# First attention of a two-layer trunk, worked by pairs of heads: values in 512-column chunks, q and k in squares of four tiles, three of eight of them in seven products

## The chip, the cores and the metric

The kernel runs on one core of one Trainium2 chip. The metric is the device time of one execution in microseconds. Three runs of the kernel before took 2495.29, 2496.64 and 2497.62 us; the median is 2496.64.

## The reference

A trunk of two layers on x of 256 positions and 2048 channels, all in float32. Layer 0 mixes tokens with differential attention, layer 1 with a dilated window attention; each is followed by a gated feed-forward block with a convolution of width 3. The change is in layer 0's attention alone:

```python
qkv = h @ w_qkv                      # 256 x 2048 by 2048 x 6144; h = rmsnorm(x)
q, k, v = jnp.split(qkv, [nqk, 2 * nqk], axis=-1)     # nqk = 2048
q = rmsnorm(q.reshape(B, S, N_HEADS, 2, HEAD_DIM), q_gain)   # 8 heads, 2 maps, 128
k = rmsnorm(k.reshape(B, S, N_HEADS, 2, HEAD_DIM), k_gain)
v = v.reshape(B, S, N_HEADS, V_DIM)                          # 256 a head
...
logits = jnp.einsum('bqhme,bkhme->bhmqk', qb, k) * scale + bias[:, None]
logits = jnp.where(dist >= 0, logits, NEG)
p = jax.nn.softmax(logits, axis=-1)
a = p[:, :, 0] - lam_full * p[:, :, 1]
... jnp.einsum('bqhk,bkhe->bqhe', a, v)
o = rmsnorm(o, subln_g) * (1.0 - lam_init)
return o.reshape(B, S, ATTN_WIDTH) @ w_o
```

## The kernel before, in words

**Products.** A float32 product is made of three matmuls on a fast type: a number is the sum of a high part and a low part, and high by high, low by high and high by low are added up. The 256 positions are two blocks (m = 0, 1) of 128. xT holds x transposed, in both parts. Weights come in chunks through four slots: SyncE issues the load into w_raw, ScalarE makes the high part w_hi (`split`, `split_up`, `split_b`; "hi split" below), VectorE subtracts to get w_lo ("lo split"), and TensorE multiplies. A chunk's raw slot is loaded anew when its low part is made (`free_slot`), its high part is overwritten when TensorE has used the chunk (`used`). Each engine has one list of instructions and works it in order, so where an instruction stands in it is part of the schedule.

**Chunks.** A plain chunk of 2048 columns costs TensorE 24 matmuls of 512 columns. In the up and down projections and in the second attention, chunks are "squares": 256 rows of x by 1024 columns of weights in four tiles. A square with 24 matmuls is `std`. For the rows in MIXED, pairs 4 to 6 of eight, a square is done in seven products in place of eight (Strassen's scheme in Winograd's form): an entry `one` of 9 matmuls from three of the loaded tiles, and an entry `sum` of 12 from four tiles that VectorE adds up (`sum_tiles`, three operations) in another slot, with no load of its own. These use mixed blocks of x (`mix_x`, `mix_high`, `mix_low`), and their products gather in four banks of PSUM that are combined after the last (`combine`).

**The first attention, before** (`a_head`, per head h, eight heads, the middle six in a loop). Chunks 0 to 3 are q and k of one head, 4 x 128 columns by 512 rows, 24 matmuls of 512 columns each. Chunks 4 to 7 are its v, 256 columns, 24 matmuls of 256 columns each. q and k gather in banks 0 and 1, v in banks 2 and 3, the attention's own results in banks 4 to 7. While a head's chunks run, the attention of the head before is done in between, by `a_attend` at the chunks in A_STEPS = (0, 2, 3, 6): scores after chunk 0; transposes of the differences of probabilities after chunk 2; P x V after chunk 3; transposes of the normed output after chunk 6. q and k of the head itself are transposed after chunk 7. VectorE adds bias, takes the maximum and, behind ScalarE's exponentials, subtracts the two maps (`a_softmax`). The norms of o and of the next head's q and k share one chain of inverse root (`a_norms`).

**The second attention** (`b_head`) has four plain chunks and eleven entries of squares, the list THREE, per head: 279 matmuls of 512 columns.

**After the last head** the output projection (`out_proj`) has 16 chunks of 24 matmuls; chunk j of the first eight needs head j of oT, in two parts (`split_o` on ScalarE and VectorE). The last head's attention is done in between, at A_LAST_STEPS = (0, 2, 3, 5).

## Time and profile before

| | us |
|---|---|
| median of three runs | 2496.64 |
| the profiled execution, span from its first to its last instruction | 2494.1 |
| TensorE busy in the span | 2487.8 |
| VectorE busy | 2100.0 |
| ScalarE busy | 1464.0 |
| GpSimd busy | 44.3 |

The profile gives the profiled execution's span; what lies around it is not in it. The median of the runs is 2.5 us longer than the span. TensorE's granted clock is 9 or more tenths of full speed in all of 40 equal slices. The 16 DMA engines move 491 MB, at 197 GB/s in the mean. The chain that ended last runs on TensorE for 98% of the span. The first attention lies at about 10 to 312 us of the span, its output projection from there to about 402, the heads of the second attention at about 1113 to 1680.

### The profile page before, as it was taken

To read this page: it belongs to the slowest core of one execution; us is meant where nothing else is said; L and a number is where in the kernel's file an instruction comes from. 1 tells how busy PE (TensorE), PEld (TensorE's weight loads), DVE (VectorE), ACT (ScalarE), POOL (GpSimd) and SP (SyncE) were. 2 spreads that over 40 slices of the span, in tenths; PEclk is the share of its full clock that TensorE was granted. 3 is DMA by queue.
4 is the path that set the end of the run, shared out by engine and by line. 5 is a ranking of instruction groups with operands and counts; after the bars stand their busy time and mean duration, and the time that the engine had idled before them with its cause. 6 is when DMAs were issued, how large, how long until landed. Compare 5 with 4: busy or idle time off the path is not lost.

```text
span 2494.1 us, 30623 instructions
## 1 busy us (share of the span) xinstructions
PE 2487.8 (100%) x11823; PEld 2088.7 (84%) x11823; DVE 2100.0 (84%) x2387; ACT 1464.0 (59%) x1561; POOL 44.3 (2%) x54
## 2 busy tenths in 40 slices
PE   9999999999999999999999999999999999999999
PEld 8988888888888888888888888888888888888887
DVE  6656666999999999998778878776699999999998
ACT  5545555766767566556545545545566676766654
POOL 1000000000000000000000000000000000000000
PEclk9999999999999999999999999999999999999999
DMA  8554554757667557476556666654476666755754
GB/s 283 180 164 162 177 198 139 247 192 248 207 214 225 193 187 244 169 227 196 157 161 188 188 190 195 185 164 152 149 251 204 220 221 206 234 186 200 240 174 159
DMA packets 364820, 491.16 MB, mean 197 GB/s; under 512 B 19285, under 2 KB 216101, under 8 KB 362256
## 3 DMA queue, kind: packets, MB, share of 16 engines
q1 hardware_dynamic: 360448, 465.64, 56.5%
q0 software_dynamic: 4000, 23.63, 4.3%
q8 instruction: 86, 1.41, 0.2%
q14 instruction: 46, 0.38, 0.0%
q10 hardware_dynamic: 240, 0.10, 0.0%
HBM read 468.31 MB, written 3.68 MB: 189 GB/s over the span
## 4 chain that ended last, share of the span: by engine, by line
PE 98%; DVE 1%; ACT 0%; DMA 0%; issue 0%; ACTq 0%
PE psum L1945 43%; PE psum L1949 22%; PE psum L1831 8%; PE psum L1832 8%; PE psum L1838 8%; PE psum L2048 2%; PE psum L1958 1%; PE psum L1957 1%; PE psum L1956 1%; PE psum L2175 1%; PE psum L1787 0%; PE psum L2139 0%; PE psum L2173 0%; PE psum L2147 0%; PE psum L2159 0%; DVE w_lo L1116 0%
## 5 line engine op out<-in xcount | busy, mean ns | idle before, releaser
L1945 PE MATMUL psum<-w_hi,xT 128*128 128x512 f32 x3936 | 984.7, 390 | 0.0
L666 ACT ACTIVATE w_hi<-w_raw 128x2048 fp32r<-128x2048 f32 (+1 forms) x350 | 631.5, 1810 | 397.3 <-PE psum L1949 262.8
L1945 PEld LDWEIGHTS psum<-w_hi,xT 128*128 128x128 f32 x3936 | 736.6, 188 | 151.8
L1116 DVE TENSOR_TENSOR w_lo<-w_raw,w_hi 128x2048 fp32r<-128x2048 f32 (+1 forms) x332 | 705.3, 2145 | 55.7 <-ACT w_hi L666 55.4
L1949 PE MATMUL psum<-w_lo,xT 128*128 128x512 f32 x1968 | 516.0, 389 | 0.1
L1949 PEld LDWEIGHTS psum<-w_lo,xT 128*128 128x128 f32 x1968 | 369.3, 188 | 77.5 <-DVE w_lo L1116 1.0
L1831 PE MATMUL psum<-w_hi,xT 128*128 128x512 f32 (+1 forms) x1008 | 362.0, 369 | 0.0
L1832 PE MATMUL psum<-w_hi,xT 128*128 128x512 f32 (+1 forms) x1008 | 355.9, 363 | 0.0
L1124 DVE TENSOR_TENSOR w_lo<-w_raw,w_hi 128x2048 fp32r<-128x2048 f32 (+1 forms) x118 | 255.7, 2179 | 41.0 <-ACT w_hi L679 40.6
L679 ACT ACTIVATE w_hi<-w_raw 128x2048 fp32r<-128x2048 f32 (+1 forms) x118 | 215.3, 1830 | 102.7 <-PE psum L1949 63.1
L1945 PE MATMUL psum<-w_hi,mixT 128*128 128x512 f32 x896 | 239.6, 389 | 0.0
L1106 DVE TENSOR_TENSOR w_lo<-w_raw,w_hi 128x2048 fp32r<-128x2048 f32 (+1 forms) x98 | 188.7, 1941 | 58.6 <-ACT w_hi L655 58.1
L1838 PE MATMUL psum<-w_lo,xT 128*128 128x512 f32 (+1 forms) x1008 | 221.8, 362 | 0.0
L1831 PEld LDWEIGHTS psum<-w_hi,xT 128*128 128x128 f32 x1008 | 190.3, 189 | 29.0 <-DVE phase L1613 0.3
L1832 PEld LDWEIGHTS psum<-w_hi,xT 128*128 128x128 f32 x1008 | 190.4, 189 | 28.6
L1838 PEld LDWEIGHTS psum<-w_lo,xT 128*128 128x128 f32 x1008 | 174.2, 189 | 29.3
L1945 PEld LDWEIGHTS psum<-w_hi,mixT 128*128 128x128 f32 x896 | 168.2, 188 | 35.0
L655 ACT ACTIVATE w_hi<-w_raw 128x2048 fp32r<-128x2048 f32 (+1 forms) x98 | 157.4, 1630 | 20.0 <-PE psum L1838 7.7
L1142 DVE TENSOR_TENSOR w_raw<-w_raw 128x1024 f32<-128x1024 f32 x112 | 136.4, 1218 | 3.5 <-DMA w_raw<-in_f_w_down 3.2
L1949 PE MATMUL psum<-w_lo,mixT 128*128 128x512 f32 x448 | 138.0, 389 | 0.0
L1949 PEld LDWEIGHTS psum<-w_lo,mixT 128*128 128x128 f32 x448 | 84.1, 188 | 17.5
L882 ACT ACTIVATE phase<-psum,conv 128x256 f32<-128x256 f32 x176 | 82.3, 571 | 5.4 <-PE psum L2048 5.2
(201 smaller groups left out, 1919.1 us busy)
## 6 DMA issues: line engine op xcount, KB each, us to landing
w_raw<-in_f_w_up SPq DMA_DIRECT2D x352, 512.0 KB, 5.1
w_raw<-in_f_w_down SPq DMA_DIRECT2D x176, 512.0 KB, 5.1
w_raw<-in_b_w_qkv SPq DMA_DIRECT2D x192, 256.0 KB, 3.9
w_raw<-in_a_w_qkv SPq DMA_DIRECT2D x94, 512.0 KB, 4.4
w_raw<-in_b_w_qkv SPq DMA_DIRECT2D x256, 128.0 KB, 2.6
w_lo<-w_raw POOLq DMA_DIRECT2D x18, 1024.0 KB, 7.0
w_raw<-in_a_w_o SPq DMA_DIRECT2D x16, 1024.0 KB, 5.1
w_raw<-in_b_w_qkv SPq DMA_DIRECT2D x32, 512.0 KB, 6.2
```

What stands on the lines that cost most here:

```text
L655: nc.scalar.activation(w_hi[:, slot, 0:width], w_raw[:, slot, 0:width], ACT.Copy).then_inc(hi_ready, 1)
L666: nc.scalar.activation(w_hi[:, slot, cols], w_raw[:, slot, cols], ACT.Copy).then_inc(hi_ready, 1)
L679: nc.scalar.activation(w_hi[:, slot, cols], w_raw[:, slot, cols], ACT.Copy).then_inc(hi_ready, 1)
L1106: nc.vector.tensor_tensor(w_lo[:, slot, 0:width], w_raw[:, slot, 0:width], w_hi[:, slot, 0:width], ALU.subtract).then_inc(lo_ready, 1)
L1116: nc.vector.tensor_tensor(w_lo[:, slot, cols], w_raw[:, slot, cols], w_hi[:, slot, cols], ALU.subtract).then_inc(lo_ready, 1)
L1124: nc.vector.tensor_tensor(w_lo[:, slot, cols], w_raw[:, slot, cols], w_hi[:, slot, cols], ALU.subtract).then_inc(lo_ready, 1)
L1142: chain.step(nc.vector.tensor_tensor(t[:, 0:2, :], b[:, 1::2, :], b[:, 0:1, :].to_broadcast([P, 2, 512]), ALU.add))
L1831: pe.matmul(o, xh, hi, start=(first and i == 0), stop=False)
L1832: pe.matmul(o, xl, hi, start=False, stop=False)
L1838: ins = pe.matmul(psum[:, banks[m], 0:n], xT[:, k, 0, P * m:P * (m + 1)], lo, start=False, stop=(last and i == len(blocks) - 1))
L1945: pe.matmul(o, x[:, h, P * m:P * (m + 1)], hi, start=start and h == 0, stop=False)
L1949: return pe.matmul(o, x[:, 0, P * m:P * (m + 1)], part_of(w_lo, c % SLOTS, 512 * tile, 512), start=False, stop=stop)
```

## The change

The eight heads are worked as four pairs. For each pair (`a_pair`) there are 15 entries: four plain chunks "all" that hold v of both heads, 512 columns by 512 rows; then squares for q and k of both heads, whose four tiles are 256 rows by the 512 columns of one head and the 512 of the other. Squares 4, 5 and 6 of eight are done as `one` and `sum`. A pair's own banks and the other four change places with each pair; v gathers in two of the own banks, then the squares in all four, and the attention of the pair before works in the other four until the `one` and `sum` products of this pair need them.

The attention (`a_attend`) is now done for two heads at once, at A_STEPS = (2, 3, 5, 6, 8): transposes of q and k after entry 2, scores after 3, transposes of the differences after 5, P x V after 6, transposes of the normed output after 8. The first `sum` entry (entry 10) waits until both takes of oT are done. In the output projection the steps of the last pair are (1, 2, 4, 4, 5), and chunks 6 and 7 need its two last heads. The loop over heads is gone from every engine's list. The norms of o have their own inverse root. The mixed blocks of x are made for the first attention too, in the first pair.

```diff
+A_ENTRIES = tuple(("all", j) for j in range(4)) + (
+    ("std", 0), ("std", 1), ("std", 2), ("one", 4), ("std", 3), ("one", 5), ("sum", 4), ("sum", 5), ("one", 6), ("sum", 6),
+    ("std", 7))
...
-A_STEPS = (0, 2, 3, 6)
-A_LAST_STEPS = (0, 2, 3, 5)
+A_STEPS = (2, 3, 5, 6, 8)
+A_LAST_STEPS = (1, 2, 4, 4, 5)
```

ScalarE:

```diff
+            def a_attend(j, p, steps, base):
+                if j == 0:
+                    a_squares(p)
                 if j == steps[0]:
+                    a_take_q(p, base)
                 if j == steps[1]:
+                    a_exp(p)
+                if j == steps[2]:
+                    a_take_aT(p, base)
                 if j == steps[3]:
+                    a_square_o(p, base)
+                    a_norm_o(p, base)
+                if j == steps[4]:
+                    a_take_oT(p, base)
```

VectorE:

```diff
+            def a_attend(j, p, steps, base):
+                if j == 0:
+                    a_norm(p)
                 if j == steps[0]:
+                    a_take_k(p, base)
+                if j == steps[1]:
+                    a_softmax(p, base)
+                if j == steps[1] + 1:
+                    a_subtract(p)
                 if j == steps[3]:
+                    dve.wait_ge(a_osq_ready, p + 1)
+                    rsqrt(o_r, o_ss, o_t, [(slice(0, 4), 1.0 / VD)], a_o_rstd)
+                if j == steps[4]:
+                    dve.wait_ge(a_to, p + 1)
+                    nc.vector.tensor_scalar(a_oT[:, 4 * p + 1:4 * p + 4:2, :],
...
+            def a_pair(c, p, odd):
+                for e in range(A_PAIR):
+                    if p == 0 and e < 2:
+                        take_xT(0, G_MIX, 2 + e)
+                        split(c + e + LEAD)
+                    if e == 3:
+                        a_take_v(c + e, p, odd)
+                    if e + LEAD + 1 == A_ONES[0]:
+                        add_weights(c + A_ONES[0], c + A_SUMS[0])
+                    if p > 0 or e > 0:
+                        split_ahead(c, e, AO0)
+                    for one, to in zip(A_ONES[1:], A_SUMS[1:]):
+                        if e + LEAD + 2 == one:
+                            add_weights(c + one, c + to)
+                    if p == 0:
+                        begin(0, G_MIX, e)
...
+                            mix_x(0)
...
                     else:
+                        a_attend(e, p - 1, A_STEPS, 4 - 4 * odd)
+                    if p == A_PAIRS - 1 and e == 11:
+                        for hd in range(4):
+                            split_o(a_oT, hd)
+                    if e == A_PAIR - 2:
+                        a_combine(c + A_SUMS[-1], p, odd)
+                    if e == A_PAIR - 1:
+                        a_sum(c + e, p, odd)
```

TensorE:

```diff
+                if what == "std" and j == 0:
+                    def lower_free():
+                        pe.wait_ge(a_v_act, p + 1)
+                        pe.wait_ge(a_v_dve, p + 1)
...
+                    if e == A_SUMS[0] and p > 0:
+                        pe.wait_ge(a_oT_act, p)
+                        pe.wait_ge(a_oT_dve, p)
+                    a_entry_of(c + e, e, p, odd)
...
+                        a_attend(e, p - 1, A_STEPS, 4 - 4 * odd)
```

`split_ahead(c, e, end)` makes the part of entry e + 3. How the rows stand on an engine, at the places of which the prediction speaks:

VectorE before, from the scores of one head to the differences (a_diff) and the next lo split; L1299 and L1302 add the bias, L1321 makes the differences.

```order
L1302 SCALAR_TENSOR_TENSOR phase<-psum,phase 128x256
L1306 TENSOR_REDUCE small<-phase 128x2 [waits a_lg_ready]
L1307 TENSOR_REDUCE small<-phase 128x2
L252 ISA
L1309 TENSOR_SCALAR small<-small 128x4 [waits dve_chain]
L1311 RECIPROCAL small<-small 128x4 [waits a_probs]
```

VectorE in the changed kernel, the same place for a pair; L1318 to L1321 take the maxima, L1139 to L1144 add up weights for entry 10, L1121 is the lo split of entry 7, L1325 is where the subtraction begins.

```order
L1318 TENSOR_REDUCE small<-phase 128x4 [waits a_lg_ready]
L1319 TENSOR_REDUCE small<-phase 128x4
L1321 TENSOR_SCALAR small<-small 128x8 [waits dve_chain]
L1139 TENSOR_TENSOR w_raw<-w_raw 128x1024 [waits w_lo_ready,w_in2]
L1142 TENSOR_TENSOR w_raw<-w_raw 128x512 [waits dve_chain]
L1144 TENSOR_TENSOR w_raw<-w_raw 128x512 [waits dve_chain]
L1121 TENSOR_TENSOR w_lo<-w_raw,w_hi 128x1536 [waits w_hi_ready]
L1325 RECIPROCAL small<-small 128x8 [waits a_probs]
L1327 TENSOR_SCALAR small<-small,nlam 128x4 [waits dve_chain]
```

Between the maxima and the reciprocal, which waits for the exponentials, stand four operations on weights that were behind the subtraction before. ScalarE in the changed kernel, from the exponentials (L756) through the squares of o (L771), its scaling (L779) and the hi splits (L678) to the take of oT (L785).

```order
L756 ACTIVATE phase,small<-phase,small 128x256 x3
L756 ACTIVATE phase,small<-phase,small 128x128 x4
L678 ACTIVATE w_hi<-w_raw 128x1536 [waits w_used,w_in2]
L678 ACTIVATE w_hi<-w_raw 128x2048 [waits w_used,w_in3]
L763 ACTIVATE phase<-psum 128x768 [waits a_ta]
L678 ACTIVATE w_hi<-w_raw 128x1536 [waits w_used,w_in0]
L771 ACTIVATE phase,small<-psum 128x256 [waits a_pv]
L771 ACTIVATE phase,small<-psum 128x256 x3
L779 ACTIVATE phase<-psum,small 128x256 [waits a_o_rstd]
L779 ACTIVATE phase<-psum,small 128x256 x3
L678 ACTIVATE w_hi<-w_raw 128x2048 [waits w_used,w_sum_ready] x2
L785 ACTIVATE phase<-psum,sub_g 128x2x256 [waits a_to]
```

The hi split of entry 7 (1536 columns) stands right behind the exponentials, and the hi splits of entries 10 and 11 between the scaling and the take. VectorE from the end of the inverse root of o to its take of oT (L1354).

```order
L1121 TENSOR_TENSOR w_lo<-w_raw,w_hi 128x2048 [waits w_hi_ready] x2
L1139 TENSOR_TENSOR w_raw<-w_raw 128x1024 [waits w_lo_ready,w_in3]
L1142 TENSOR_TENSOR w_raw<-w_raw 128x512 [waits dve_chain]
L1144 TENSOR_TENSOR w_raw<-w_raw 128x512 [waits dve_chain]
L1354 TENSOR_SCALAR phase<-psum,sub_g 128x2x256 [waits a_to]
```

The take stands behind two lo splits (entries 10 and 11) and the sum for entry 13. VectorE at the start, behind the inverse root of x: before, then in the changed kernel (L1264 and L1258 are the first take of q and k, and of v).

```order
L1723 COPY gains<-psum 128x10 [waits pe_setup,r_rstd]
L1725 COPY conv<-psum 128x352 x2
L1106 TENSOR_TENSOR w_lo<-w_raw,w_hi 128x1024 [waits w_hi_ready]
L1733 ISA phase,small<-phase 128x128 [waits lam_in]
L1733 ISA small 128x1
L1733 ISA phase,small<-phase 128x128
L1733 ISA small 128x1
L1737 TENSOR_SCALAR sub_g<-gains 128x2 [waits consts_ready]
L1740 TENSOR_SCALAR nlam<-small 128x1 [waits lam_exp]
L1264 TENSOR_SCALAR phase<-psum,small 128x512 [waits w_used,lam_ready]
```

```order
L1743 COPY gains<-psum 128x10 [waits pe_setup,r_rstd]
L1745 COPY conv<-psum 128x352 x2
L1153 TENSOR_TENSOR phase<-phase 128x384 [waits xT_hi]
L1154 TENSOR_TENSOR phase<-phase 128x384
L1156 TENSOR_TENSOR phase<-phase 128x384 [waits dve_chain]
L1158 TENSOR_TENSOR phase<-phase 128x384 [waits dve_chain]
L1258 TENSOR_SCALAR phase<-psum,small 128x512 [waits w_used]
L1121 TENSOR_TENSOR w_lo<-w_raw,w_hi 128x2048 [waits w_hi_ready]
```

The four mixing operations stand ahead of the take now, and the take is of v.

## Rows read from the trace of the kernel before

**Rows 1.** The table by stage: a head of the first attention, one of the second (columns: stretch and its length; then for PE, PEld, DVE, ACT, POOL busy us (instructions); clock, DMA share, GB/s).

```profile
86.40:124.04 37.64, 37.64 (x225) 33.46 (x223) 23.29 (x39) 19.47 (x43) 0.00 (x0) 1.00 0.52 168
1269.50:1341.08 71.58, 71.58 (x337) 60.01 (x336) 56.56 (x62) 36.70 (x32) 2.38 (x2) 1.00 0.61 178
```

**Rows 2.** PE in order of time: start, length, line, operands.

```profile
82.96 0.28 PE L1831 MATMUL psum<-w_hi,xT 128*128 128x256 f32 x1
83.08 0.28 PE L1832 MATMUL psum<-w_hi,xT 128*128 128x256 f32 x1
...
86.94 0.40 PE L1831 MATMUL psum<-w_hi,xT 128*128 128x512 f32 x1
87.17 0.40 PE L1832 MATMUL psum<-w_hi,xT 128*128 128x512 f32 x1
```

**Rows 3.** DVE in order of time, within one head of the first attention.

```profile
131.24 0.69 DVE L1299 SCALAR_TENSOR_TENSOR phase<-psum,phase 128x512 f32<-128x512 f32 x1 [2.10 <-PE psum L1864]
...
133.34 0.17 DVE L1309 TENSOR_SCALAR small<-small 128x4 f32<-128x4 f32 x1
135.45 0.18 DVE L1311 RECIPROCAL small<-small 128x4 f32<-128x4 f32 x1 [1.94 <-ACT phase L767]
...
137.25 3.43 DVE L1106 TENSOR_TENSOR w_lo<-w_raw,w_hi 128x2048 fp32r<-128x2048 f32 x2
...
152.58 0.24 DVE L1197 TENSOR_SCALAR small<-small 128x8 f32<-128x8 f32 x2 [1.83 <-ACT phase L745]
```

**Rows 4.** ACT in order of time, within the same head.

```profile
133.55 0.51 ACT L763 ACTIVATE phase<-phase,small 128x256 f32<-128x256 f32 x1 [6.73 <-DVE small L1309]
...
135.32 2.85 ACT L655 ACTIVATE w_hi<-w_raw 128x2048 fp32r<-128x2048 f32 x2
...
151.73 0.36 ACT L745 ACTIVATE phase<-psum 128x256 f32<-128x256 f32 x1
...
152.44 1.05 ACT L655 ACTIVATE w_hi<-w_raw 128x1024 fp32r<-128x1024 f32 x1
155.11 0.84 ACT L780 ACTIVATE phase<-psum,small 128x256 f32<-128x256 f32 x2 [1.62 <-DVE small L1211]
155.84 3.72 ACT L655 ACTIVATE w_hi<-w_raw 128x2048 fp32r<-128x2048 f32 x2
```

**Rows 5.** DVE in order of time, within one head of the second attention.

```profile
1359.13 4.09 DVE L1124 TENSOR_TENSOR w_lo<-w_raw,w_hi 128x1536 fp32r<-128x1536 f32 x2 [0.30 <-ACT w_hi L679]
1363.15 1.22 DVE L1142 TENSOR_TENSOR w_raw<-w_raw 128x1024 f32<-128x1024 f32 x1
...
1365.73 0.42 DVE L1671 COPY phase<-psum 128x256 f32<-128x256 f32 x1
```

**Rows 6.** DVE in order of time, in the first head.

```profile
30.76 1.23 DVE L1106 TENSOR_TENSOR w_lo<-w_raw,w_hi 128x1024 fp32r<-128x1024 f32 x1 [1.09 <-ACT w_hi L655]
...
34.55 0.95 DVE L1725 COPY conv<-psum 128x352 f32<-128x352 f32 x2
...
37.58 0.75 DVE L1264 TENSOR_SCALAR phase<-psum,small 128x512 f32<-128x512 f32 x1
```

**Rows 7.** PE in order of time, the end of the fourth chunk.

```profile
34.22 1.98 PE L1838 MATMUL psum<-w_lo,xT 128*128 128x512 f32 x8
```

**Rows 8.** Instructions of one line: the mixing of x.

```profile
L1156 DVE TENSOR_TENSOR phase<-phase x3: 547/548/548, 416.9 to 1792.9; 128x384 f32<-128x384 f32 x3
```

**Rows 9.** PE in order of time, at the start.

```profile
1.20 4.41 PE L2261 MATMUL psum<-phase 128*128 128x128 f32 x22 [1.20 <-DVE phase L1744]
6.48 0.63 PE L1787 MATMUL psum<-ident,resid 128*128 128x128 f32 x4 [0.87 <-DMA resid<-in_x]
...
8.07 1.50 PE L2261 MATMUL psum<-phase 128*128 128x128 f32 x12
```

**Rows 10.** The table by stage, the end of the span.

```profile
2491.00:2493.00 2.00, 0.00 (x0) 0.00 (x0) 0.64 (x1) 0.00 (x0) 0.00 (x0) 1.00 0.59 224
2493.00:2494.10 1.10, 0.00 (x0) 0.00 (x0) 0.00 (x0) 0.00 (x0) 0.00 (x0) 0.54 0.19 69
```

More of the change, by code:

```diff
@@ L28 @@
 import math
-from contextlib import ExitStack, contextmanager
+from contextlib import ExitStack
 import numpy as np
@@ L95 @@
 A0 = 0
-AO0 = A0 + H * A_HEAD
+AO0 = A0 + A_PAIRS * A_PAIR
 UP0 = (AO0 + OUT, 0)
@@ L145, in loads_of @@
     if A0 <= c < AO0:
-        return 2 if (c - A0) % A_HEAD < 4 else 1
+        return {"all": 1, "sum": 0}.get(kind(c), 4)
     if B0 <= c < BO0:
@@ L469, in load_x, with free_slot, load_a_pair @@
                 sp.dma_start(resid[:, :, cols], src).then_inc(x_in[q], 16)
-            def free_slot(c, more=None):
-                if more is None:
-                    lo_made(sp, c - SLOTS)
-                else:
-                    at_least(sp, lo_ready, c - SLOTS + 1 + more)
-            def load_a_head(c, h, more=0):
-                for j in range(A_HEAD):
-                    first = isinstance(h, int) and j < 4
+            def free_slot(c):
+                lo_made(sp, c - SLOTS)
+            def load_a_pair(c, p):
+                for e, (what, j) in enumerate(A_ENTRIES):
+                    if what == "sum":
+                        continue
+                    first = p == 0 and e < 4
@@ L647, in _, with split @@
         def _(act):
-            def split(c, more=0, width=W, rate=RATE):
+            def split(c):
                 if c >= END:
@@ L839, in out_proj @@
                     split(c + j + LEAD)
-                    if j < 5:
-                        split_o(oT, oT_act, oT_dve, j + 2)
-                    if j == 3 and n == 1:
-                        a_squares(H)
-                    attend(j, H - 1, steps)
+                    if early + j < H - group:
+                        split_o(oT, oT_act, oT_dve, early + j, group)
+                    attend(j, last, steps, base)
                     if j == steps[-1]:
-                        split_o(oT, oT_act, oT_dve, H - 1)
+                        for hd in range(H - group, H):
+                            split_o(oT, oT_act, oT_dve, hd, group)
                     if j == 7:
@@ L1098, in _, with split @@
             chain = Chain(dve, dve_chain)
-            def split(c, more=0, width=W):
+            def split(c):
                 if c >= END:
@@ new lines, in a_sum, with a_norm @@
+            def a_sum(c, p, odd):
+                chunk_used(dve, c)
+                dve.wait_ge(a_combined, p + 1)
+                for i in range(2 * M):
+                    nc.vector.tensor_tensor(a_raw[:, i, :], psum[:, a_bank(odd) + i, :], a_raw[:, i, :],
+                                            ALU.add).then_inc(a_summed, 1)
+            def a_norm(p):
+                dve.wait_ge(a_sq_ready, p + 1)
+                rsqrt(q_r, q_ss, q_t, [(slice(0, 16), 1.0 / HD)], None)
+                chain.settle()
+                r = q_r.rearrange("p (g m s) -> p g m s", m=M, s=4)
+                chain.step(nc.vector.tensor_tensor(
+                    r, r, r_r.unsqueeze(1).unsqueeze(3).to_broadcast([P, 2, M, 4]), ALU.mult))
+                chain.settle()
+                v = a_raw.rearrange("p m (s e) -> p (m s) e", e=HD)
+                nc.vector.tensor_tensor(v, v, q_r.unsqueeze(2).to_broadcast([P, 16, HD]), ALU.mult).then_inc(a_qkn, 1)
@@ L1366, in a_head @@
-                    if j == 7:
-                        a_take_v(c + j, h, more)
-                        split(c + j + LEAD, more)
-                        a_take_k(h)
+                            mix_low(0)
+                    else:
+                        a_attend(e, p - 1, A_STEPS, 4 - 4 * odd)
+                    if p == A_PAIRS - 1 and e == 11:
+                        for hd in range(4):
+                            split_o(a_oT, hd)
+                    if e == A_PAIR - 2:
+                        a_combine(c + A_SUMS[-1], p, odd)
```

680 lines of the change are left out of this document (319 added, 361 removed).

## The prediction

> **What bounds the kernel now.** I read the table by stage first. Over one head of the first attention TensorE is busy for all of its 37.64 us, VectorE for 23.29 and ScalarE for 19.47; over one head of the second attention TensorE is busy for all of 71.58 us and VectorE for 56.56 [rows 1]. So TensorE's own work is the whole time, and every wait that others keep from it is worth nothing until it grows past its cover. The second view is the order of matmuls in time, for the distance from one start to the next: 0.12 us at 256 columns and 0.23 at 512 [rows 2]; over a run of 512-column matmuls I use 0.227. The third is the order in time of VectorE and ScalarE within one head [rows 3, 4] and in one head of the second attention [rows 5], for the pieces of the chains that the change makes longer.
>
> **What TensorE saves.** The value projections were 192 matmuls of 256 columns for two heads and become 96 of 512: 192 x 0.120 - 96 x 0.227 = 1.25 us a pair. Q and k were 192 matmuls of 512 columns for two heads; now five plain squares of 24, three "one" entries of 9 and three "sum" entries of 12 make 183: 9 x 0.227 = 2.04 us. Together 3.3 us a pair, 13.2 us over four pairs. The attention's own small matmuls stay the same in number. Half of the interludes go, which I cost at 0.1 to 0.5 us in all and leave out. Had the 256-column matmul been as fast per column as the 512-column one, 0.114 instead of 0.12, the first term would be zero and the sum 8.2.
>
> **Steady pairs: the softmax chain.** Let 0 be the end of the scores of the pair before. PE (its entries 4 and 5) then has 2 x 24 x 0.227 = 10.9 us of weights' work before it asks for the differences (a_diff). What it asks for takes, with everything that stands in the queues between:
> VectorE's lo split of entry 6 ends 0.45 us after the scores, because it had to stand behind the take of v;
> two softmax fronts, 2 x (133.34 - 131.24) = 4.2 us [rows 3];
> two sets of exponentials on ScalarE, 2 x (135.32 - 133.55) = 3.55 us [rows 4];
> then ScalarE's hi split of entry 7 (1536 columns, three quarters of 3.72/2, so 1.4) [rows 4] and VectorE's lo split of the same (4.02 to the next start for one of 1536 and one of 2048, so 1.75 and 2.25) [rows 5]: both stand ahead of the subtraction in VectorE's list, and the hi stands behind the exponentials in ScalarE's;
> two subtractions, 2 x (137.25 - 135.45) = 3.6, less the reciprocal and one small multiply that do not double, 2.9 us [rows 3].
> The sum is 14.2 us against 10.9: TensorE waits 3.3 us. The weight sum for entry 10 (2.58 us, [rows 5]) lies beside the exponentials and costs nothing. Before, one head's chain (6.0 us from 131.24 to 137.25) had the same cover.
>
> **Steady pairs: the output chain.** From the end of P x V TensorE has entry 7 (9 matmuls, 2.04), entry 8 (24, 5.45), eight transposes (0.9; one comes 0.11 after another, from 12 in 1.50 [rows 9]) and entry 9 (2.04) = 10.4 us until entry 10, which waits for a_oT_dve. The chain: 0.25 to notice; four squares of o, 2 x (152.44 - 151.73) = 1.4 [rows 4]; the inverse root, 155.11 - 152.58 = 2.5 [rows 3, 4]; four scalings, 2 x (155.84 - 155.11) = 1.5 [rows 4]; hi split of entry 10, 3.72/2 = 1.86 [rows 4]; lo splits of 10 and 11, 2 x 2.25 [rows 5]; the weight sum for entry 13, 1365.73 - 1363.15 = 2.58 [rows 5]; and only then the take of oT by VectorE, 0.75, as the 512-column take from PSUM in [rows 6]. That is 15.3 us: TensorE waits 4.9. The transposes in the middle are met: the scaling ends 5.7 us after P x V, TensorE comes at 7.5.
>
> Both waits come once in pairs 1, 2 and 3: 3 x (3.3 + 4.9) = 24.6 us. A 1024-column operation might cost anything from one head's time to twice it; with softmax front and subtraction at 1.7 instead of 2 the waits are 0.3 x 3.9 = 1.2 us a pair less, and with 0.1 us more at each of some ten handovers 1 us more: 21 to 28 us.
>
> **The first pair.** Its values lie in banks 0 and 1, which the lower half of entry 4 overwrites, so TensorE waits there for VectorE's take of v. Before, the take of the first chunks' result ended at 38.3 (37.58 + 0.75) [rows 6] and the next chunk, in other banks, did not need it. Ahead of it stands the inverse root of x, which started at 32.0 behind a lo split (30.76 + 1.23) [rows 6]. Now ScalarE makes six extra copies of x (0.4 each, about 1 us of them outside its idle time) and two full hi splits in place of half ones (1.9), and the last lo split is full too (1.1): the root starts near 36. Then the root, 2.5 [rows 3, 4]; the constants, 0.95 [rows 6]; four new mixing operations of 0.55 [rows 8]; the take, 0.75: 42.4. TensorE ends the fourth chunk at 34.22 + 8 x 0.227 = 36.0 as before [rows 7] and has 12 matmuls (2.7 us) that need no bank of v: a wait of 3.7 us, say 4, between 2 and 6.
>
> **The last attention,** inside the output projection, has the steps 1, 2, 4, 4, 5. The softmax chain is as above with a hi and lo split of 2048 columns: 4.1 us of wait. Differences and P x V share a step, so the take of the transposed probabilities is bare, 1.1. Its first chunk waits for the combination, pushed back by four split_o on VectorE, and the transposes of q and k for their norms: 1.5. Chunk 6 needs oT of the same step: the rest of a hi split 0.95, a lo split 2.2, take 0.75, split_o on both engines (512 columns, 0.65 each, a little under the take) 1.3 = 5.2; before, a chunk lay between. The o norms lack 0.4. Together 12 us, between 7 and 15.
>
> **The clock.** In the stages of [rows 1] TensorE never waits, and the granted clock is 1.00. In its last stretch TensorE does nothing for 2 us from 2491 and the granted clock is then 0.54 [rows 10], its lower level (1.2 GHz) for nearly all of it. At the start 22 warming matmuls take 4.41 us where 12 take 1.50 once it is warm, so 22 would take 2.6: the climb costs 1.8 us [rows 9]. All nine large waits (4.0; 3 x 3.3 and 3 x 4.9; 4.1 and 5.2) are longer than 2 us. I charge 1.8 to the six long ones and half to the three of 3.3: 13.5 us, between 0 and 18.
> The Trainium skill, "TensorE: Matmul & The Clock Gate", section "HAM oscillation — how this bites in real kernels", says that a kernel which keeps TensorE waiting between bursts pays the climb again in every round; the last stretch agrees that idleness lowers the clock, but no wait inside this kernel shows it. By the page the charge is the upper end, 9 x 1.8 = 16 us; without it zero.
>
> **The sum,** against the profiled execution (span 2494.1; the median of the timed runs, 2496.6, lies 2.5 above it, and I put that on top): 2494.1 - 13.2 + 24.6 + 4 + 12 + 13.5 + 2.5 = 2537.5. Work of the other engines elsewhere, loads (the same bytes) and the later stages I cost at nothing: VectorE is at 79% in the second attention's heads with the same split and sum entries, and TensorE doesn't wait there.
>
> **Rivals.**
> A. The waits come, the clock stays up: 2524. For it: 0.87 us of idleness near the start did not bring the lower level back (the matmuls behind it are not slower) [rows 9]. Against it: 2 us at the end did.
> B. Only part of the waits. Were oT taken in time, by VectorE's queue running ahead of what I add up, 3 x (4.9 + 1.8) = 20 us go: 2517. Against it: the list is in order, and the take stands behind both lo splits and the sum.
> C. All is covered, as in the second attention: 2494.1 - 13.2 + 2.5 = 2483. For it: the same form of head runs there without a wait. Against it: there one head's softmax, not two heads', stands in each step, and oT is taken right after P x V with no norm between.
> D. VectorE becomes the bound of whole pairs: 46.6 us for two heads before, plus 7.7 for three weight sums, up to 6 for eight combining operations of at most 0.75, and 2.5 for a second inverse root, is about 63 of 72; were gaps in its order to cost 5 us a pair over my sum: 2552.
>
> **Chances.** Forecast 0.5; A 0.2; B 0.12; D 0.08; C 0.1. The range from 2508 to 2550 leaves out C and part of D. About 0.2% (5 us) is what a measurement of this kernel can tell from no change. Faster comes with C alone: 0.08; within 0.2%, with half of the waits of B and no fall of the clock: 0.03; slower: 0.89. Should it be faster, C's condition decides: both waits of a steady pair under 1 us.
>
> **What would show it.** A pair of heads lasts 3.3 us less than 75.3 with no waits, 80 to 84 with them. PE's idle time is led by the transposes of the differences, released by VectorE's subtraction, and by the first sum entry, released by the take of oT, three times each, then by entry 4 of the first pair and by chunk 6 of the output projection. The matmuls behind a wait stand 0.43 apart if the clock fell. If TensorE's idle time in the first attention is under 10 us, my chains are wrong; if it is 40 and the time 2524, only the clock is.

## The result, and the profile after

The changed kernel takes 2544.5 us (median of four runs, 2541.1 to 2545.9); the kernel before, on the same chip, 2496.0 (2495.2 to 2497.6). The ratio is 1.0193, with a 95% interval of 1.0179 to 1.0208. The forecast was 2537.5, between 2508 and 2550.

The page of the kernel after, its engines and its chain:

```profile
PE 2496.5 (98%) x11403; PEld 2075.8 (82%) x11403; DVE 2155.9 (85%) x2389; ACT 1484.1 (58%) x1544; POOL 44.3 (2%) x54
...
PE 92%; DVE 4%; ACT 2%; issue 1%; DMA 1%; SPq 0%; ACTq 0%; DVEq 0%
```

TensorE's busy time has grown by 8.7 us, though products were taken from it, and is still 98% of a span of 2543.9 us. Of the chain it holds 92% where it held 98%, so the page hints at the loss but does not place it. All of the loss comes ahead of the first gated feed-forward block. VectorE's first mixing of x for that block, before and then after, starts 49.7 us later, and the whole span is 49.8 us longer:

```profile
416.94 0.55 DVE L1156 TENSOR_TENSOR phase<-phase 128x384 f32<-128x384 f32 x1
```

```profile
466.60 0.55 DVE L1153 TENSOR_TENSOR phase<-phase 128x384 f32<-128x384 f32 x1
```

The table of waits shows where, for TensorE over the first 430 us (engine, line it waited at, what released it; us in all, times, longest):

```profile
PE psum L1979 <- issue: 14.4, 3, 4.8
PE psum L1882 <- DVE phase L1335: 12.7, 4, 3.7
PE psum L1990 <- DVE conv L1745: 5.6, 1, 5.6
PE psum L1846 <- DVE xT L1400: 5.1, 1, 5.1
PE psum L1866 <- DVE phase L1291: 2.1, 1, 2.1
...
PE psum L1888 <- ACT phase L763: 0.9, 1, 0.9
```

In the order of the rows: the first sum entry of pairs 1 to 3, which waits for the transposed o (the releaser is not named here; the rows of VectorE below do it); the transposes of the softmax differences, three times 3.0 in pairs and once 3.7 beside the output projection; entry 4 of the first pair; chunk 6 of the output projection; the last transposes of q and k; the last transposed probabilities. They are 40.8 us. Two more, of 0.5 us behind the last pair and 0.2 us at the transposes of the last o, bring them to 41.5; 2.0 us of waits at the very start, which the kernel before has too (2.4 there), are not counted. In the kernel before, TensorE was busy for the whole of a head [rows 1]. Now, in the table by stage, pairs 1 and 2 (each from its q and k transposes to the next pair's), and the stretch behind the wait for o in pair 1:

```profile
100.83:186.61 85.78, 77.97 (x339) 64.27 (x338) 60.05 (x79) 43.18 (x80) 0.00 (x0) 0.92 0.46 148
186.61:269.15 82.54, 74.72 (x339) 61.80 (x338) 60.05 (x79) 43.19 (x80) 0.00 (x0) 0.96 0.47 153
151.00:157.80 6.80, 6.16 (x15) 4.83 (x16) 4.41 (x3) 2.43 (x2) 0.00 (x0) 0.50 0.91 305
```

Pair 1 lasts 85.78 us and pair 2 82.54; two heads took 2 x 37.64 = 75.28 [rows 1]. In pair 2 TensorE is busy for 74.72 us, at 0.96 of the clock: only one of its two waits brought the clock down. In pair 1 both did. The third row lies at 0.50 for its whole length. What that does to a matmul, and what the wait looks like, is seen in TensorE's order of time at that place:

```profile
151.65 2.90 PE L1979 MATMUL psum<-w_hi,mixT 128*128 128x512 f32 x6 [4.80 <-issue]
154.34 1.05 PE L1979 MATMUL psum<-w_hi,xT 128*128 128x512 f32 x2
```

The wait is 4.80 us (in brackets). Behind it six matmuls of 512 columns take 2.90 us, where at full clock they start 0.23 apart [rows 2]. VectorE at the same time:

```profile
143.80 4.49 DVE L1121 TENSOR_TENSOR w_lo<-w_raw,w_hi 128x2048 fp32r<-128x2048 f32 x2 [3.44 <-ACT w_hi L678]
148.21 1.22 DVE L1139 TENSOR_TENSOR w_raw<-w_raw 128x1024 f32<-128x1024 f32 x1
...
150.80 0.74 DVE L1354 TENSOR_SCALAR phase<-psum,sub_g 128x512 f32<-128x512 f32 x1
```

Two lo splits in one row, the three operations of a weight sum (the first is shown), and only then the take of the transposed o (L1354), which ends at 151.54: 0.1 us later TensorE goes on. This is the row for row form of the chain that was added up ahead. The other chain, on VectorE, for the softmax of the same pair:

```profile
120.17 1.76 DVE L1121 TENSOR_TENSOR w_lo<-w_raw,w_hi 128x1536 fp32r<-128x1536 f32 x1 [2.49 <-ACT w_hi L678]
121.84 0.20 DVE L1325 RECIPROCAL small<-small 128x8 f32<-128x8 f32 x1
...
122.21 1.00 DVE L1331 TENSOR_SCALAR phase<-phase,small 128x128 f32<-128x128 f32 x4
123.25 1.40 DVE L1335 SCALAR_TENSOR_TENSOR phase<-phase,small 128x128 f32<-128x128 f32 x4
```

The lo split of entry 7 stands ahead of the reciprocal and the subtractions, which end at 124.65; TensorE goes on at 124.7.

In the first pair the releaser is not the one that I had named. VectorE there:

```profile
37.28 0.15 DVE L1215 TENSOR_REDUCE small<-small 128x2 f32<-128x8 f32 x1
...
39.92 0.95 DVE L1745 COPY conv<-psum 128x352 f32<-128x352 f32 x2
...
42.91 0.74 DVE L1258 TENSOR_SCALAR phase<-psum,small 128x512 f32<-128x512 f32 x1
```

The order is: split of entry 5, inverse root from 37.28, the copy of the constants (the last of it L1745) which ends at 40.87, four mixing operations (in the gap), and the take of v at 42.91. TensorE's entry 4 starts at 40.93, 0.06 us behind the copy.

### The profile page after: what moved, and what is told of

It is laid out like the page before. It is cut to its first block, busy times and chain, and to the rows that moved or that the text cites. A ratio compares the mean times of both kernels' runs of the same rounds, so it can differ in the third digit from the quotient of the medians.

```text
span 2543.9 us, 29223 instructions
## 1 busy us (share of the span) xinstructions
PE 2496.5 (98%) x11403; PEld 2075.8 (82%) x11403; DVE 2155.9 (85%) x2389; ACT 1484.1 (58%) x1544; POOL 44.3 (2%) x54
## 4 chain that ended last, share of the span: by engine, by line
PE 92%; DVE 4%; ACT 2%; issue 1%; DMA 1%; SPq 0%; ACTq 0%; DVEq 0%
PE psum L1979 46%; PE psum L1983 23%; PE psum L1846 5%; PE psum L1847 5%; PE psum L1853 5%; PE psum L2082 2%; PE psum L1990 1%; PE psum L1992 1%; PE psum L1991 1%; PE psum L2209 1%; DVE w_lo L1121 1%; DMA w_raw<-in_a_w_qkv 1%; ACT phase L756 0%; PE psum L2173 0%; PE psum L2207 0%
## 5 line engine op out<-in xcount | busy, mean ns | idle before, releaser
L1979 PE MATMUL psum<-w_hi,xT 128*128 128x512 f32 x4264 | 1073.8, 392 | 0.0
L1979 PEld LDWEIGHTS psum<-w_hi,xT 128*128 128x128 f32 x4264 | 801.4, 189 | 165.5
L665 ACT ACTIVATE w_hi<-w_raw 128x2048 fp32r<-128x2048 f32 (+1 forms) x350 | 631.0, 1809 | 397.1 <-PE psum L1983 254.9
L1113 DVE TENSOR_TENSOR w_lo<-w_raw,w_hi 128x2048 fp32r<-128x2048 f32 (+1 forms) x332 | 705.0, 2145 | 58.4 <-ACT w_hi L665 57.6
L1983 PE MATMUL psum<-w_lo,xT 128*128 128x512 f32 x2132 | 560.3, 390 | 0.1
L1983 PEld LDWEIGHTS psum<-w_lo,xT 128*128 128x128 f32 x2132 | 400.5, 188 | 84.1 <-DVE w_lo L1113 1.0
L1121 DVE TENSOR_TENSOR w_lo<-w_raw,w_hi 128x2048 fp32r<-128x2048 f32 (+1 forms) x174 | 376.3, 2177 | 79.9 <-ACT w_hi L678 79.5
L678 ACT ACTIVATE w_hi<-w_raw 128x2048 fp32r<-128x2048 f32 (+1 forms) x174 | 316.8, 1828 | 157.5 <-PE psum L1983 100.2
L1979 PE MATMUL psum<-w_hi,mixT 128*128 128x512 f32 x992 | 270.3, 395 | 14.4 <-issue 14.4
L1846 PE MATMUL psum<-w_hi,xT 128*128 128x512 f32 x624 | 247.4, 396 | 5.7 <-DVE xT L1400 5.1
L1847 PE MATMUL psum<-w_hi,xT 128*128 128x512 f32 x624 | 244.5, 392 | 0.0
L1979 PEld LDWEIGHTS psum<-w_hi,mixT 128*128 128x128 f32 x992 | 189.3, 191 | 55.4 <-issue 15.6
L1853 PE MATMUL psum<-w_lo,xT 128*128 128x512 f32 x624 | 154.2, 389 | 0.0
L1139 DVE TENSOR_TENSOR w_raw<-w_raw 128x1024 f32<-128x1024 f32 x124 | 151.1, 1219 | 0.9 <-DMA w_raw<-in_f_w_down 0.8
L1846 PEld LDWEIGHTS psum<-w_hi,xT 128*128 128x128 f32 x624 | 118.3, 190 | 30.7 <-DVE xT L1400 5.4
L1847 PEld LDWEIGHTS psum<-w_hi,xT 128*128 128x128 f32 x624 | 118.2, 189 | 24.0
L1853 PEld LDWEIGHTS psum<-w_lo,xT 128*128 128x128 f32 x624 | 117.1, 188 | 24.3
L1103 DVE TENSOR_TENSOR w_lo<-w_raw,w_hi 128x2048 fp32r<-128x2048 f32 x38 | 86.0, 2288 | 34.1 <-ACT w_hi L654 34.1
L1142 DVE TENSOR_TENSOR w_raw<-w_raw 128x512 f32<-128x512 f32 x124 | 85.8, 692 | 4.2
L1144 DVE TENSOR_TENSOR w_raw<-w_raw 128x512 f32<-128x512 f32 x124 | 85.8, 692 | 4.2
```

Of the source, the lines that this page charges most:

```text
L665: nc.scalar.activation(w_hi[:, slot, cols], w_raw[:, slot, cols], ACT.Copy).then_inc(hi_ready, 1)
L678: nc.scalar.activation(w_hi[:, slot, cols], w_raw[:, slot, cols], ACT.Copy).then_inc(hi_ready, 1)
L1103: nc.vector.tensor_tensor(w_lo[:, slot, :], w_raw[:, slot, :], w_hi[:, slot, :], ALU.subtract).then_inc(lo_ready, 1)
L1113: nc.vector.tensor_tensor(w_lo[:, slot, cols], w_raw[:, slot, cols], w_hi[:, slot, cols], ALU.subtract).then_inc(lo_ready, 1)
L1121: nc.vector.tensor_tensor(w_lo[:, slot, cols], w_raw[:, slot, cols], w_hi[:, slot, cols], ALU.subtract).then_inc(lo_ready, 1)
L1139: chain.step(nc.vector.tensor_tensor(t[:, 0:2, :], b[:, 1::2, :], b[:, 0:1, :].to_broadcast([P, 2, 512]), ALU.add))
```

## The experiments

All are edits of the changed kernel; the comments in the edits below are the document's, and "..." stands for rows left out. "Gap" is the distance between the starts of two matmuls, which is 0.2 us or so more than the idle time in the tables. Time at the low clock is added up from the table by stage, asked for in stretches of half a microsecond over the first 430 us: it is 0 in the kernel before and 54.6 us in the changed one, in nine stretches. Each starts within one of the large waits or up to 1.5 us behind it.

**TensorE kept busy through its waits.** This version separates what the waits cost from what the clock behind them costs.

```diff
+ def spin(turns, bank):
+     for i in range(turns):
+         pe.matmul(psum[:, bank, 0:P], ident[:, :], ident[:, :], start=True, stop=True)
...
...
+ spin(15, base + 3)          # ahead of pe.wait_ge(a_diff, p + 1)
+ spin(24, 4)                 # first pair, ahead of pe.wait_ge(consts_ready, 1)
+ spin(22, 5 - 4 * odd)       # ahead of pe.wait_ge(a_oT_act, p)
+ spin(22, 5)                 # output projection, ahead of chunk 6
```

> TensorE is given idle products (fp32 identity by identity, 128 columns, written to a bank that is free) to run while it would wait: 15 calls (about 3.3 us) ahead of each wait for the subtraction of the softmax, 22 (about 4.9 us) ahead of the three waits for the transposed o of a pair and ahead of chunk 6 of the output projection, 24 (about 5.3 us) ahead of the wait for the constants in the first pair. The waits themselves stay as long as they are; only the engine is not idle in them. The wait of 2.5 us ahead of the last q and k transposes is left as it is. Theory A (the clock that falls after a wait costs about 19 us of the 50 that the change costs): eight of the nine falls are gone, one of about 3.4 us is left, and the time is 2525 to 2529 us, 1.012 of the time before. Theory B (my prediction's size of the clock term, 13.5 us, is right, and the remaining loss is longer waits): 2531 to 2533. Theory C (the clock falls whatever the engine does there, or the low clock costs nothing): 2543 to 2546, falls still at the same places.

Measured: 2526.4 us (2526.2 to 2527.3), ratio 1.0118 [1.0101, 1.0135]; no time at the low clock. TensorE at the place shown above:

```profile
142.10 5.07 PE L1860 MATMUL psum<-ident 128*128 128x128 f32 x44
147.06 1.63 PE L1988 MATMUL psum<-w_hi,mixT 128*128 128x512 f32 x6
```

The 22 calls are 44 records, 5.07 us long, and the six matmuls behind them take 1.63 us in place of 2.90. The waits are all still there, filled: no other instruction was moved. The wait ahead of the last q and k transposes was left empty (1.6 us here), and the clock stayed up behind it. This is Theory A: the clock costs 2544.5 - 2526.4 = 18.1 us and not 13.5, and the waits proper the rest. Between the two profiled executions it is 2543.9 - 2524.3 = 19.6, since that of the changed kernel was 1.2 us above its median. Rival A's picture, waits without the clock, is what this run makes, and its 2524 is 2 us from it.

**The subtraction first.**

```diff
  for e in range(A_PAIR):
+     if p > 0 and e in (4,):
+         a_attend(e, p - 1, A_STEPS, 4 - 4 * odd)
      if p > 0 or e > 0:
          split_ahead(c, e, AO0)
...
-     else:
+     elif e not in (4,):
          a_attend(e, p - 1, A_STEPS, 4 - 4 * odd)
```

> Only VectorE's order in pairs 1 to 3 changes: the subtraction of the softmax stands ahead of the split of the weights of entry 7, not behind it. Theory A (the wait of 3.4 us behind entry 5 is VectorE's order: the subtraction stood behind a 1.8 us split that itself waited for ScalarE's copy): the three waits of 3.2 us net shrink to under 0.4, TensorE comes to the next wait earlier by as much, and the wait for the transposed o stays 5.0 to 5.4, since VectorE's and ScalarE's work for it hangs on TensorE's own progress; with the falls of the clock behind two of the three waits gone the time is 2530 to 2534. Theory B (the backlog only moves: VectorE or ScalarE is what is short over the pair): the wait for o grows to about 8, the pair stays 82.4 us long and the time 2542 to 2545. Theory C (the exponentials on ScalarE end last): the wait shrinks by at most 1.5 us each, time 2539 to 2541.

Measured: 2527.6 us (2527.5 to 2528.8), ratio 1.0122 [1.0105, 1.0139]; 37.6 us at the low clock. The wait for o in the three pairs, then two waits behind the last pair:

```profile
PE psum L1981 <- issue: 14.4, 3, 4.8
...
PE psum L1868 <- DVE phase L1291: 1.6, 1, 1.6
PE psum L1848 <- DVE phase L1272: 0.9, 1, 0.9
```

The three waits for the differences are gone, and the wait for o has stayed at 4.8. Theory A, with more gained than it said: 17 us, 9 of them these waits and 0.7 the first pair's, which is 4.9 here, though the edit does not touch that pair. The low clock fell from 54.6 us to 37.6, which by the run above (18.1 us for 54.6) is worth 5.6. The remaining 1.6 us are not assigned.

**The take of o first.** The same edit with 8 in place of 4.

> Only VectorE's order in pairs 1 to 3 changes: its half of the copy of the transposed o out of PSUM stands ahead of the split of entry 11's weights and of the sums of entries 12 and 13, not behind them. Theory A (the 5.2 us wait at the first product of sums is VectorE's order; what it waits for would be ready otherwise): the three waits go to under 0.6, the falls of the clock behind them go too (2.3 us each), and the time is 2521 to 2526. Theory B (the chain of o itself is late: square, 1/sqrt, scale, transposes, with ScalarE's copy as the last): the waits shrink to about 2.6 to 3 and the clock still falls, time 2536 to 2540. Theory C (the work put off, split and sums, is then what TensorE waits for at entries 11 to 13): a new wait of 3 us or more there, time 2540 or more.

Measured: 2531.7 us (2529.5 to 2535.9), ratio 1.0141 [1.0124, 1.0158]; 37.5 us at the low clock. Waits of the three pairs and at the start of the output projection, and VectorE in order of time:

```profile
PE psum L1884 <- DVE phase L1335: 9.0, 3, 3.0
PE psum L1848 <- DVE phase L1272: 4.8, 1, 4.8
PE psum L1848 <- DVE phase L1267: 3.3, 2, 2.4
```

```profile
142.31 2.29 DVE L1121 TENSOR_TENSOR w_lo<-w_raw,w_hi 128x2048 fp32r<-128x2048 f32 x1 [3.44 <-ACT w_hi L678]
144.52 0.74 DVE L1354 TENSOR_SCALAR phase<-psum,sub_g 128x512 f32<-128x512 f32 x1
...
162.95 0.68 DVE L1267 TENSOR_TENSOR phase<-psum,phase 128x512 f32<-128x512 f32 x1
```

Theory A is right about the wait named: 14.4 us are gone, the take now stands at 144.52, between the lo splits. But 8.1 us came back at a place that none of the three theories had: the start of the chunk that follows a pair, the next pair's twice (2.4 and 0.9 us) and the output projection's once (4.8, where the changed kernel has 0.5). This chunk needs banks that VectorE must first have read for the combination (L1267 to L1272). VectorE comes to it at 162.95, behind splits for which it had waited 0.32 and 1.79 us on ScalarE. ScalarE itself was waiting for weights:

```profile
154.71 1.92 ACT L678 ACTIVATE w_hi<-w_raw 128x2048 fp32r<-128x2048 f32 x1 [0.89 <-DMA w_raw<-in_a_w_qkv]
158.79 1.92 ACT L678 ACTIVATE w_hi<-w_raw 128x2048 fp32r<-128x2048 f32 x1 [2.16 <-DMA w_raw<-in_a_w_qkv]
```

A slot is loaded anew only when its low part is made, so a low part that is late delays a load as well. How much of the 8.1 us goes this way no run takes apart. What had stood ahead of the take was put off, and TensorE, no longer held at entry 10, reached the pair's end earlier than VectorE. The gain is 12.8 us where 18 to 23 were expected.

**Both.**

> Both moves on VectorE in pairs 1 to 3: the subtraction ahead of the split of entry 7, and the copy of the transposed o ahead of the split of entry 11 and the sums. Each alone gave 17 and 13 us; in the second the wait came back at the start of the next pair (2.8, 1.3 and 5.1 us, until VectorE had combined the products of the pair before). Theory A (two waits of their own, and the new one is the splits put off, which does not grow): 17 and 13 add to 30, time 2513 to 2517. Theory B (backlog: with 3.2 us less of TensorE time ahead of it, VectorE is later yet against TensorE at the pair's end): the wait for the combine grows by up to 3 us a pair, time 2519 to 2525. Theory C (with VectorE free of it the wait at the first product of sums is the chain of o and comes back there): waits of 2.5 us there, 2519 or more.

Measured: 2520.6 us (2517.0 to 2523.8), ratio 1.0092 [1.0076, 1.0107]; 34.1 us at the low clock.

```profile
PE psum L1848 <- DVE phase L1267: 6.8, 2, 3.4
PE psum L1848 <- DVE phase L1272: 4.8, 1, 4.8
```

The gains do not add (24 us in place of 30). Theory B: the wait for the combination grew from 8.1 to 11.6 us over the three. A cause for it is in the row at 142.31 above: the lo split of entry 10 waits 3.44 us for ScalarE's high half, which stands behind the scaling of o, and this in turn behind VectorE's inverse root. That is tried below, with all the other edits.

**The constants first, in the first pair.** take_consts is called at e == 2 ahead of split_ahead and not behind the inverse root.

> First pair only: VectorE copies the constants out of PSUM before it splits the weights of entry 5, not after the 1/sqrt. My prediction held the split, the sum and the take of v responsible for a 4 us wait at entry 4; the trace after names the copy of the constants, 5.6 us. Theory A (constants): the wait ahead of entry 4 disappears, its upper half runs, and then TensorE waits for the scaled v in the middle of entry 4 for about 4.3 us, ScalarE's or VectorE's part last: total gain 1 to 2 us, time about 2543. Theory B (something else holds entry 4 at its start, a transfer or the split of its own weights): the wait at its start stays over 3 us.

Measured: 2540.1 us, one run; 41.0 us at the low clock. TensorE in entry 4:

```profile
42.67 0.47 PE L1991 MATMUL psum<-w_hi,xT 128*128 128x512 f32 x1 [4.34 <-DVE phase L1258]
```

The wait at the entry's start is gone; L1991 is in its middle, and the wait there is for the take of v (L1258), 4.34 us. Theory A, to the tenth in the wait. Of the total it said 1 to 2 us and 4.4 came: 1.3 us of wait, and the low clock is 13.6 us shorter, which by the rate above would be up to 4.5. But the changed kernel's own runs lie 4.8 us apart, so the total of one run decides little.

**Constants, inverse root and v first.** take_consts, begin and a_take_v are all called at e == 2 of the first pair ahead of the split.

> First pair only: VectorE does the constants, 1/sqrt and its half of the scaled v first, and then the split of entry 5, mix_x and the rest. Moving the constants alone left a 4.7 us gap in the middle of entry 4 until v had been copied behind mix_x (2.1 us) and the split (2.3 us). Theory A (order again): no gap over 1 us in entry 4, no low clock behind it, and the time is 4.3 us of wait plus 1.4 to 2 us of clock below the version with the constants alone: 2533 to 2536. Theory B (the split of entry 5 or the mixed x that are put off come too late): a wait of 2 us or more in entry 5 or at the first entry of mixed products, time 2538 or more.

Measured: 2536.3 us, one run; 41.0 us at the low clock. TensorE has no idle time at all between 33 and 45 us. Theory A on the wait, with a time 0.3 us above its range; of the clock nothing came back, since the one stretch that is gone here was made up by others that were longer. One run of each kernel carries no more than that.

**The tail's order.** Only the last attention, beside the output projection:

```diff
  for j in range(OUT):                       # VectorE; ScalarE with j == 5 alone
+     first = n == 1 and j in (3, 5)
+     if first:
+         attend(j, last, steps, base)
+         if j == 5:
+             for hd in range(H - group, H):
+                 split_o(oT, hd)
      split(c + j + LEAD)
...
```

> Only the last attention, beside the output projection: VectorE subtracts ahead of the split of chunk 5, and both VectorE and ScalarE copy the transposed o and split it for chunk 6 ahead of the weights of chunk 7. Theory A (order): the 4.1 us gap goes to under 0.5, the 5.4 us gap to 2.2 to 2.8 (VectorE's copy 0.75, ScalarE's 0.6 of high halves, VectorE's 0.65 of low halves and the semaphores are left), and one or two of the three clock falls go: 2 to 4 us; time 2533 to 2537. Theory B (chunk 7 is late in turn, or the exponentials end last): 2540 or more, with a new gap at chunk 7 or the old one at the transposes of the probabilities.

Measured: 2531.8 us (2531.5 to 2532.0), ratio 1.0142 [1.0126, 1.0157]; 34.1 us at the low clock, none of it behind the last pair. Waits of the tail:

```profile
PE psum L1859 <- DVE xT L1406: 2.3, 1, 2.3
PE psum L1879 <- DVE phase L1297: 1.6, 1, 1.6
```

The 3.7 us for the differences are gone, and chunk 6 waits 2.3 in place of 5.1. Theory A on the waits; the time is 1.2 us under its range of 2533 to 2537. All three falls behind the last pair are gone (17.1 us at the low clock, 5.7 by the rate above) where it had expected one or two.

**All together:** both moves in pairs 1 to 3, the constants, inverse root and v first in the first pair, and the tail's order, with ScalarE's high half of entry 10 between the squares of o and its scaling, and 9 idle products ahead of chunk 6:

```diff
  if j == steps[3]:
      a_square_o(p, base)
+     if between is not None:
+         between()                          # split_ahead(c, 7, AO0): the high half of entry 10
      a_norm_o(p, base)
```

> All moves together: both in pairs 1 to 3, ScalarE's high half of entry 10 between the squares of o and its scaling in place of behind it, constants and v first in the first pair, the tail's order, and 9 idle products (2 us) ahead of chunk 6. If every wait but the last transposes' (2.0), the probabilities' in the tail (1.1), chunk 6's (2.3) and one of about 1 a pair is gone, 43.5 us of waits come down to 9 and the low clock with them (54.6 us of it in the change, under 7 here): 2494.1 - 13.2 + 9 + 2 = 2492 in a profile, 2494 as a median, the same as before within 0.2%. Theory A (the removed products are worth their 13 us once order hides the waits): 2490 to 2497. Theory B (VectorE's backlog at the pair's end stays): 3 waits of 3 to 5 us with their clock, 2503 to 2512.

Measured: 2493.5 us (2491.9 to 2498.1, 11 runs) against 2496.5, ratio 0.9990 [0.9981, 0.9999]; 6.8 us at the low clock. Its two longest waits behind the start:

```profile
PE psum L1867 <- DVE phase L1280: 3.8, 1, 3.8
...
PE psum L1913 <- ACT phase L763: 0.9, 1, 0.9
```

The waits for the combination that the run with both moves had in pairs 1 and 2 are gone (the one of 0.5 us in the changed kernel is back), and ScalarE's high half of entry 10 is the only edit that these pairs have beyond that run. Between 95 and 310 us VectorE's lo splits waited 17.1 us for ScalarE in that run and wait 1.2 here, so the lateness began there. The first pair, ahead of them, was edited too; no run has the high half moved alone. One is left, 3.8 us behind the last pair, where four split_o and two splits of the projection's weights stand ahead of it. Theory A.

**The last combination first.** In the last pair alone a_combine goes ahead of the split of the projection's chunk 0, a_sum ahead of that of chunk 1, and ScalarE's copy of the first product ahead of the high half of chunk 1.

> The version with all moves had one wait left, 4.2 us between the last pair and the output projection, until VectorE had combined the last products (it stood behind two splits of the projection's weights), and one fall of the clock behind it. Here, in the last pair only, ScalarE copies the first product before it makes the high half of the projection's chunk 1, and VectorE combines ahead of the split of chunk 0 and adds ahead of that of chunk 1. Theory A (order again): the wait goes to under 0.5, about 1 comes back at the next transposes of q and k (now 1.3 us of margin, of which 4.2 go and 2 come back), no fall of the clock: 4 us of wait less, 2 to 3 of clock less, 1 more: 2486 to 2489, 0.3 to 0.4% under the time before. Theory B (the splits put off are late in chunk 0 or 1 of the projection): a gap of 2 us or more there, 2491 to 2494.

Measured: 2491.9 us (2489.5 to 2496.5, 11 runs) against 2496.8, ratio 0.9984 [0.9975, 0.9993]; no low clock in the profiled run. Its waits, and two steady pairs in the table by stage:

```profile
PE psum L1897 <- DVE phase L1301: 3.1, 1, 3.1
...
PE psum L1919 <- ACT phase L763: 0.9, 1, 0.9
PE psum L1873 <- DVE phase L1277: 0.5, 1, 0.5
PE psum L1873 <- DVE xT L1420: 0.3, 1, 0.3
```

```profile
93.93:166.00 72.07, 72.07 (x339) 60.06 (x338) 59.87 (x79) 43.08 (x80) 0.00 (x0) 1.00 0.54 176
166.00:238.09 72.09, 72.09 (x339) 60.11 (x338) 60.03 (x79) 43.09 (x80) 0.00 (x0) 1.00 0.54 175
```

The wait moved to the next transposes of q and k (3.1 us where 1 was expected), which is 2 of the 3 to 6 us by which the median lies above the 2486 to 2489 expected. Neither theory fits it fully. The time lies in Theory B's range (2491 to 2494), but the splits put off were not late; the norm of q and k behind the sum is (L1301 releases the wait).

**Without the idle products.**

> The same without the 9 idle products ahead of chunk 6 of the projection: TensorE idles about 2.3 us there. Theory A (a lone wait of 2 to 2.6 us was not followed by a low clock in the version with the tail's order alone, while in the changed kernel one of 2.5 us close behind others was): the time is that of its twin within 1 us. Theory B (every wait of 2 us and more is followed by a fall): one fall of 3.4 to 6.8 us, 1.2 to 2.5 us slower than its twin.

Measured: 2493.3 us (2490.7 to 2495.6, 11 runs), ratio 0.9985 [0.9976, 0.9994].

```profile
PE psum L1893 <- DVE phase L1301: 3.1, 1, 3.1
PE psum L1873 <- DVE xT L1420: 2.3, 1, 2.3
```

By time it is undecided. The medians are 1.4 us apart, outside the 1 us of Theory A and within the 1.2 to 2.5 of Theory B, but the runs of either version spread over 5 to 7 us and the two intervals against the kernel before are nearly the same. The profiled run speaks for B: the low clock was there, 10.2 us of it, 3.4 of them at the wait of 2.3 us. The other 6.8 stand at the wait of 3.1 us, where its twin kept the full clock.

## Why the prediction was right

The direction, the places and nearly all sizes came from adding up the lists of instructions between two handovers.

**What TensorE saves:** 3.3 us a pair was forecast. The last version shows pairs in which TensorE is never idle and at full clock: 72.07 and 72.09 us against 75.28 [rows 1], so 3.2. The saving is real; the waits and the clock cost more than four times as much.

**Softmax chain:** 3.3 a pair, measured 3.0 idle, 3.4 from start to start. Undoing its one ingredient that the order chose (the split ahead of the subtraction) took all of it away, so the chain's remaining length fits beneath the 10.9 us of cover.

**Output chain:** 4.9 a pair, measured 4.8. (A pair was to last 80 to 84 us: pair 2 does, pair 1 with 85.8 does not, by the clock.) Here the order alone was not enough to get it back: the take stood behind the splits because the splits were late themselves.

**First pair:** 4 us forecast, 5.6 in this profile (4.2 to 5.6 in the profiles of the five kernels that leave it as it is). The size was near, the step was wrong: "TensorE ... has 12 matmuls (2.7 us) that need no bank of v". They need the banks in which the constants lie, and these are copied behind the inverse root. The take of v (42.91 to 43.65) would have held TensorE for as long in the middle of the entry, and did when the constants were moved, so the price came out by a second way. That it was near is in part luck.

**Last attention:** 12 forecast; 3.7 + 0.9 + 2.1 + 0.5 + 5.1 + 0.2 = 12.5 measured.

**The clock** is the term that was mis-sized: 13.5 forecast, 18.1 measured by the medians and 19.6 between the profiled executions. I had given a fall 1.8 us, from the climb at the start [rows 9], and counted the three waits of 3.3 at half. Two of these three were followed by the low clock, and so was the wait of 2.1 us ahead of the last q and k transposes, which I had not counted: nine stretches at 2.0 us in the mean. The Trainium skill's rule ("TensorE: Matmul & The Clock Gate", section "HAM oscillation — how this bites in real kernels") that the climb is paid again in every round, which I had put at 16 us, was nearer than my half measure; the trace agrees with it at nine of the ten waits of 2 us and more.

**The sum:** in the profiles the change is 2543.9 - 2494.1 = 49.8 us; - 12.8 + 41.5 + 18.1 = 46.8. Of the 3 us left over 1.5 come of setting a difference of medians (18.1) among figures of profiles (19.6). The rest may be the gap from start to start, 0.2 us longer than the idle time at each of ten waits; no run shows that. The forecast's - 13.2 + 24.6 + 4 + 12 + 13.5 = 40.9 lacks the clock's 4.6, the first pair's 1.6, 0.5 at the tail, 0.4 of saving and these 3, and has 1.2 too much in the steady pairs' waits (9.0 + 14.4).

**The rivals:** A (2524) is answered by the filled waits: the clock does fall. B rested on VectorE running ahead; it came to the take of oT no sooner than my list had it. C (2483, all hidden) was wrong for the order given, and right about the work: with the lists reordered the steady pairs have no wait. D (VectorE the bound) falls with the same rows: VectorE is busy for 59.9 of 72.1 us, 3 less than I had added up, and TensorE never waits. In the steady pairs it was the order, not the amount.

The version with the last combination first is 4.9 us under the kernel before (0.16%) and not 13. Its own waits (3.1, 0.9, 0.5, 0.3, 0.2) and 2 us of idle products are 7 of the 8 us between. What stays open is which of its waits brings the clock down in which run (the mean granted clock of its eleven runs lies between 0.998 and 1.000), and so how much of its spread of 7 us that is.

## What to carry to other kernels

Where two heads share a step, the chain between two handovers nearly doubles and the cover does not; add up, for each handover, everything that stands in both engines' lists between, and hold it against the work that TensorE has in hand. What is moved ahead puts something else off (14.4 us gained at one wait, 8.1 lost at the next), so start at the earliest lateness, not at the one that TensorE feels. A wait of 2 to 6 us cost its length and, where the clock fell, on average 2 us of slow matmuls.

## What the runs showed of the hardware

The same wait does not always bring the clock down, which I had not expected. In the changed kernel the wait of 3.0 us in pair 2 (from 207 us) was followed by full clock and those in pairs 1 and 3 were not; the wait of 2.3 us ahead of chunk 6 was followed by full clock in the version with the tail's order alone, and by the low clock in the version without idle products. Behind a wait the clock is at 0.50, its lower level of 1.2 GHz, and the 512-column matmuls stand 0.43 us apart in place of 0.23.

Keeping TensorE at fp32 products of the identity (0.22 us a call, two records) through a wait was enough to hold the clock at 1.00, and it slowed neither VectorE nor ScalarE by anything that the waits show.
